# Seven products for eight in the last feed-forward layer of a fused float32 kernel

## The reference, cut to what matters

```python
h2 = rmsnorm_2(x, norm2_g[l])
g = jnp.einsum('bsd,df->bsf', h2, w_gate[l])
u = jnp.einsum('bsd,df->bsf', h2, w_up[l])
x = x + jnp.einsum('bsf,fd->bsd', jax.nn.silu(g) * u, w_down[l])
return rmsnorm_2(x, normf_g)
```

## Time and profile before

| | |
|---|---|
| median of 3 runs | 1824.84 us (1824.78 to 1824.85) |
| span of the profiled execution | 1822.8 us |
| TensorE busy | 1810.1 us, 99% of the span |
| VectorE, ScalarE, GpSimd busy | 938.6, 727.8, 272.3 us |
| the layer's first matmul starts, its last one ends | about 1451.3 and 1811.3 us |

### The profile page before, as it was taken

How to read it: one execution, slowest core, us unless ns; L and a number is a source line. 1 busy time by engine, 2 the same in 40 slices (tenths; PEclk the granted TensorE clock), 3 DMA queues, 4 the chain that set the end, 5 groups by cost and what they waited for, 6 DMA issues and landing times.

```text
span 1822.8 us, 21331 instructions
## 1 busy us (share of the span) xinstructions
PE 1810.1 (99%) x8733; PEld 1472.7 (81%) x8733; DVE 938.6 (51%) x1429; ACT 727.8 (40%) x1155; POOL 272.3 (15%) x241
## 2 busy tenths in 40 slices
...
GB/s 243 67 88 66 70 95 114 93 93 94 91 95 96 118 128 108 82 47 93 93 95 113 93 93 95 91 110 99 70 103 59 70 109 100 93 92 93 102 89 64
DMA packets 32337, 173.41 MB, mean 95 GB/s; under 512 B 4064, under 2 KB 6240, under 8 KB 14320
## 3 DMA queue, kind: packets, MB, share of 16 engines
...
...
## 4 chain that ended last, share of the span: by engine, by line
PE 96%; ACT 1%; DVE 1%; DMA 0%; POOL 0%; issue 0%; SPq 0%; ACTq 0%; DVEq 0%; POOLq 0%
PE ps L995 54%; PE ps L1299 20%; PE ps L929 7%; PE ps L1014 5%; PE ps L1141 2%; PE ps L1186 2%; PE ps L1166 2%; PE ps L1034 1%; PE ps L1225 1%; PE ps L1206 1%; DMA raw<-in_wall 0%; ACT PC L1543 0%; DVE WL L1806 0%; ACT WH L1375 0%; POOL sq L2326 0%
## 5 line engine op out<-in xcount | busy, mean ns | idle before, releaser
L995 PE MATMUL ps<-hH,WH 128*128 128x512 f32 x1456 | 570.9, 392 | 0.1
L1806 DVE TENSOR_TENSOR WL<-raw,WH 128x1024 fp32r<-128x1024 f32 (+2 forms) x308 | 377.3, 1264 | 368.1 <-ACT WH L1375 367.9
L995 PE MATMUL ps<-hH,WL 128*128 128x512 f32 x1456 | 566.7, 389 | 0.0
L995 PE MATMUL ps<-hL,WH 128*128 128x512 f32 x1456 | 566.7, 389 | 0.0
L1375 ACT ACTIVATE WH<-raw 128x1024 fp32r<-128x1024 f32 (+2 forms) x308 | 301.4, 1026 | 311.8 <-PE ps L1299 228.6
L995 PEld LDWEIGHTS ps<-hH,WH 128*128 128x128 f32 x1456 | 273.3, 188 | 65.3 <-issue 7.3
L995 PEld LDWEIGHTS ps<-hH,WL 128*128 128x128 f32 x1456 | 273.3, 188 | 57.0
L995 PEld LDWEIGHTS ps<-hL,WH 128*128 128x128 f32 x1456 | 273.3, 188 | 56.9 <-issue 1.0
L1299 PE MATMUL ps<-fL,WH 128*128 128x512 f32 x531 | 205.9, 388 | 0.0
L1299 PE MATMUL ps<-fH,WL 128*128 128x512 f32 x531 | 205.9, 388 | 0.0
L1299 PE MATMUL ps<-fH,WH 128*128 128x512 f32 x531 | 205.9, 388 | 0.0
...
## 6 DMA issues: line engine op xcount, KB each, us to landing
raw<-in_wall SPq DMA_DIRECT2D x140, 1024.0 KB, 4.6
...
```

The costliest lines, as they stand in the source:

```text
L995: mm = e.matmul(ps[b][:, 0:N], ww[:, k, c:c + 128], x[:, k, 0:N], start=(k == 0 and i == 0), stop=(k == 7 and i == 2))
L1806: e.tensor_tensor(WL[n % NCV][:, c], raw[n % NRAW][:, c], WH[n % NCV][:, c].bitcast(F32), ALU.subtract).then_inc(*mark("wl", n, x))
```

## The change

The last layer's gate and up are made as one 2x2 block product. A round s (of 11) takes 256 columns of gate and 256 of up. The blocks are: k tiles even or odd (4 each), gate or up columns, and tokens 0 to 255 or 256 to 511. The seven products (numbered 1 to 7) use the weight blocks as loaded (1, 2, 4) or sums of them (5, 6, 3, 7), made by VectorE (`wsum`) before the split, and blocks or differences of blocks of the moving side, made once per pair of k tiles in `res_norm`. Each product is 4 x 2 x 3 = 24 matmuls of 256 columns. Products 1, 6, 7, 4 add up in one PSUM bank, 5 and 3 in another, 2 in a third; ScalarE copies the partial sums out (`wcopy`) before the next product is added on top, and the next product waits for that copy. VectorE joins the copies to gate (`wc12`, `wc11`) and up (`wz1`, `wz0`).

Weights are split in chunks of 128x1024, with four places for WH/WL chunks; a chunk is converted when the chunk four before it has been used. A third raw buffer serves the layer. The down product is no longer in two halves: its parts (groups of 2, 4, 4, 4, 4 k tiles, each added to X on its own, `wx`) run between the products, and the last 4 k tiles run as the tail, `res_ffn` as before.

The plan and the order of steps (indentation of the diff is shortened here):

```diff
+WINO = (2,)
+NSU = 11
+CHUNK = 1024
+W_SLOTS = 2 * NCV
+TAIL = ((0, (0,)), (1, (1,)), (2, (2, 3)))
...
+def down_pieces(s):
+  if s == 0:
+    return []
+  if s < 3:
+    return [(0, s - 1)]
+  return [((s - 1) // 2, 2 * ((s - 1) % 2) + x) for x in (0, 1)]
...
+def wino_sequence():
+  out = []
+  for s in range(NSU):
+    q = lambda n, p0=0, p1=4, s=s: ("q", s, n, p0, p1)
+    d = [("d",) + x for x in down_pieces(s)]
+    if s == 0:
+      out += [q(1, 0, 3), q(5, 0, 3), q(2, 0, 3), q(1, 3), q(5, 3), q(2, 3), q(6), q(3), q(7),
+          ("q", 1, 1, 0, 4), q(4)]
+    elif s < 3:
+      out += ([] if s == 1 else [q(1)]) + [q(5), q(6), q(3), q(7), q(2)] + d + [q(4)]
+    else:
+      out += [q(1), q(5), q(6), q(3), d[0], q(7), q(2), d[1], q(4)]
+  return out
...
+units = [ROLE[i, "U1", s], ROLE[i, "U2", s]]
+at = block_of(q)
+if at:
+  c["unit"], c["at"] = ROLE[i, at[0], s], at[1] * CHUNK
+else:
+  c["sum"] = {5: ((units[0], CHUNK), (units[1], 0)), 6: ((i, "q", s, 5), (units[0], 0)),
+        3: ((i, "q", s, 6), (units[1], CHUNK)), 7: ((units[0], 0), (units[0], CHUNK))}[q]
+  c["place"] = {5: 0, 6: 1, 3: 0, 7: 1}[q]
+c["from"] = units[0] if q == 1 else units[1]
...
 def conv_ahead(end):
-  while now["conv"] < min(end, len(UNITS)) and (now["conv"] < NCV or now["conv"] - NCV in done):
-    for x in (0, 1):
-      put("conv", now["conv"], x)
+  while now["conv"] < len(ITEMS):
+    item = ITEMS[now["conv"]]
+    kind, n = item
+    first = n if kind == "unit" else CHUNKS[n]["from"]
+    if first >= end or any((b if b[0] == "chunk" else b[1]) not in done for b in W_BEFORE[item]):
+      return
+    if kind == "unit":
+      for x in (0, 1):
+        put("conv", n, x)
+    else:
+      for c in range(now["summed"], min(n + 2, len(CHUNKS))):
+        if CHUNKS[c]["i"] == CHUNKS[n]["i"]:
+          if CHUNKS[c]["sum"]:
+            put("wsum", c)
+          now["summed"] = c + 1
+      put("cconv", n)
     now["conv"] += 1
...
+def ffn_wino(i, end):
+  late = []
+  def used(key):
+    done.add(("chunk", CHUNK_AT[key]))
+  for at, x in enumerate(SEQUENCE):
+    conv_ahead(len(UNITS))
+    if x[0] == "d":
+      _, g, c = x
+      put("wd", i, g, c)
+      while late:
+        put(*late.pop(0))
+      used((i, "d", g, c))
+      put("wx", i, g, c)
+      continue
+    _, s, q, p0, p1 = x
+    put("wp", i, s, q, p0, p1)
+    while late:
+      put(*late.pop(0))
+    if at == 2:
+      put("rstd_rows", FFN_NORMS[i], 61 if i == 2 else 60)
+    if p1 < 4:
+      continue
+    used((i, "q", s, q))
+    if q in (1, 5, 6, 7):
+      put("wcopy", i, s, q)
+    elif q == 3:
+      put("wc12", i, s)
+    elif q == 2:
+      put("wc11", i, s)
+    if q == (3 if s == 0 else 2):
+      put("wgate", i, s)
+    if q == 4:
+      put("wz1", i, s)
+      late.append(("wz0", i, s))
+  while late:
+    put(*late.pop(0))
+  hread = ("wq", i, NSU - 1, 4)
+  if i == 2:
+    put("sqrt_table")
+  for mg in (0, 1):
+    n = ROLE[i, "T", mg]
+    now["unit"] = n + 1
+    conv_ahead(n + 2)
+    for gi, ks in TAIL:
+      for mi in range(4):
+        put("wtail", i, mg, gi, mi, n, ks)
+        if gi == 2:
+          put("res_ffn", i, 1, 4 * mg + mi, hread)
+    done.add(n)
...
-rstd("n2", 61)
+if 2 not in WINO:
+  rstd("n2", 61)
```

Places, and which moving block a product takes:

```diff
+FH = place("FH", [128, 8, 512], F32R, offset=wino)
+FL = place("FL", [128, 8, 512], F32R, offset=wino + 16384)
+raw.append(place("raw2", [128, SLOT], offset=wino + 32768))
+Wsum = [place(f"Wsum{x}", [128, CHUNK], offset=wino + 40960 + 4096 * x) for x in (0, 1)]
+held_q1, held_q5, held_v, held_w = (place(f"held{x}", [128, 2, 256], offset=wino + 49152 + 2048 * x)
+                  for x in range(4))
+TH = place("TH", [128, 4, 3, 256], F32R, offset=wino + 57344)
+TL = place("TL", [128, 4, 3, 256], F32R, offset=wino + 57344 + 12288)
+gs = place("gs", [128, 2, 512], offset=wino + 81920)
+yz = place("yz", [128, 2, 512], offset=wino + 86016)
+Tf = place("Tf", [128, 8, 256], offset=wino + 81920)
+DH = place("DH", [128, 4, 4, 256], F32R, offset=hH_at)
+DL = place("DL", [128, 4, 4, 256], F32R, offset=hL_at)
...
+def moving(q, p):
+  x = {1: 0, 2: 1, 3: 2, 4: 3, 5: 4, 6: 5, 7: 6}[q]
+  if x < 3:
+    return TH[:, p, x, :], TL[:, p, x, :]
+  return DH[:, p, x - 3, :], DL[:, p, x - 3, :]
```

TensorE:

```diff
+elif what == "wp":
+  i, st, pn, p0, p1 = a
+  c = CHUNK_AT[i, "q", st, pn]
+  kind = {1: "wA", 6: "wA", 7: "wA", 4: "wA", 5: "wD", 3: "wD", 2: "wB"}[pn]
+  opens = pn in (1, 5, 2)
+  if opens and p0 == 0:
+    b, before = bank((kind, i, st), {"wA": ("wg", "z", 0), "wD": ("wg", "c12"), "wB": ("wg", "c11")}[kind] + (i, st),
+            hold=kind == "wA")
+    if before:
+      w.wait_ge(*at(*before))
+  b = BANK[kind, i, st]
+  if not opens:
+    w.wait_ge(*at("wcopy", i, st, {6: 1, 7: 6, 4: 7, 3: 5}[pn]))
+  w.wait_ge(*at("wl", "c", c))
+  W = [x.rearrange("p (k c) -> p k c", k=4) for x in chunk_slot(c)]
+  for p in range(p0, p1):
+    w.wait_ge(*at("wg", "t", "L", i, p, int(pn > 3)))
+    H, L = moving(pn, p)
+    for u in (0, 1):
+      for n, (ww, x) in enumerate(((W[0], H), (W[0], L), (W[1], H))):
+        mm = e.matmul(ps[b][:, 256 * u:256 * u + 256], ww[:, p, 128 * u:128 * u + 128], x,
+               start=(opens and p == 0 and u == 0 and n == 0),
+               stop=(p == 3 and u == 1 and n == 2), skip_group_check=True)
+  if p1 == 4:
+    mm.then_inc(*mark("wq", i, st, pn))
+    FREED["chunk", c] = ("wq", i, st, pn)
+  if pn == 4:
+    turns.append(b)
...
+for mi, m in enumerate(part_tiles(g, part)):
+  b, before = bank(("wd", i, g, m), ("wg", "x", i, g, m))
+  if before:
+    w.wait_ge(*at(*before))
+  for kx in range(nk):
+    f = k0 + kx
+    w.wait_ge(*at("wpool", "L", i, f // 2))
+    for n, (ww, x) in enumerate(((W[0], FH), (W[0], FL), (W[1], FH))):
+      mm = e.matmul(ps[b][:, :], ww[:, kx, mi * 128:mi * 128 + 128], x[:, f % 8, :],
+             start=(kx == 0 and n == 0), stop=(kx == nk - 1 and n == 2))
+  mm.then_inc(*mark("wq", "d", i, g, m))
+  FREED["chunk", c] = ("wq", "d", i, g, m)
```

ScalarE (`cconv`, `wcopy`, the silu of `wgate`, the copy of `wz0`, `res_norm`):

```diff
+elif what == "cconv":
+  c = a[0]
+  if CHUNKS[c]["sum"]:
+    w.wait_ge(*at("wg", "sum", c))
+  else:
+    w.wait_ge(*loaded(CHUNKS[c]["unit"]))
+  for b in W_BEFORE["chunk", c]:
+    w.wait_ge(*at(*FREED[b]))
+  e.activation(chunk_slot(c)[0], chunk_src(c), ACT.Copy).then_inc(*mark("wh", "c", c))
+elif what == "wcopy":
+  i, st, pn = a
+  dst = {1: held_q1, 5: held_q5, 6: held_v, 7: held_w}[pn]
+  w.wait_ge(*at("wq", i, st, pn))
+  if st:
+    w.wait_ge(*at(*{1: ("wg", "c11"), 5: ("wg", "z", "c22"), 6: ("wg", "c12"), 7: ("wg", "z", 1)}[pn], i, st - 1))
+  e.activation(dst[:, :, :], by_tile(BANK["wD" if pn == 5 else "wA", i, st]), ACT.Copy).then_inc(
+    *mark("wcopy", i, st, pn))
+elif what == "wgate":
+  i, st = a
+  if st:
+    w.wait_ge(*at("wpool", "L", i, st - 1))
+  w.wait_ge(*at("wg", "r", i, st))
...
+e.activation(yz[:, :, :], gs[:, :, :], ACT.Silu).then_inc(*mark("wsilu", i, st))
...
+w.wait_ge(*at("wg", "z", 1, i, st))
+w.wait_ge(*at("wg", "z", 0, i, st))
+if st >= 4:
+  w.wait_ge(*at("wq", "d", i, group_of(st - 4), 7))
+f = 2 * st % 8
+e.activation(FH[:, f:f + 2, :], yz[:, :, :], ACT.Copy).then_inc(*mark("wsilu", "H", i, st))
...
+if st in WINO_OF:
+  i, p = WINO_OF[st], m // 2
+  src = X[:, m, :].rearrange("p (h t) -> p h t", h=2)
+  if p:
+    w.wait_ge(*at("wg", "t", "L", i, p - 1, 1))
+  e.activation(Tf[:, 1:3, :] if m % 2 else Tf[:, 0:8:7, :], src, ACT.Copy,
+        scale=col(st, m)).then_inc(*mark("wcopy", "t", "g", i, m))
+  if m % 2:
+    w.wait_ge(*at("wcopy", "t", "g", i, m))
+    e.activation(TH[:, p, :, :], Tf[:, 0:3, :], ACT.Copy).then_inc(*mark("wcopy", "t", "H", i, p, 0))
+    w.wait_ge(*at("wg", "t", "d", i, p, 4))
+    e.activation(DH[:, p, :, :], Tf[:, 3:7, :], ACT.Copy).then_inc(*mark("wcopy", "t", "H", i, p, 1))
+else:
+  e.activation(hH[:, m, :], X[:, m, :], ACT.Copy, scale=col(st, m)).then_inc(
+    *mark("hH", st, m))
```

VectorE (`res_norm` last):

```diff
+elif what == "wsum":
+  c = CHUNKS[a[0]]
+  src = []
+  for y in c["sum"]:
+    if len(y) == 2:
+      w.wait_ge(*loaded(y[0]))
+      src.append(raw[RAW_AT[y[0]]][:, y[1]:y[1] + CHUNK])
+    else:
+      w.wait_ge(*at("wg", "sum", CHUNK_AT[y]))
+      src.append(Wsum[CHUNKS[CHUNK_AT[y]]["place"]][:, :])
...
+  e.tensor_tensor(Wsum[c["place"]][:, :], src[0], src[1], ALU.add).then_inc(*mark("wg", "sum", a[0]))
+elif what == "cconv":
+  c = a[0]
+  H, L = chunk_slot(c)
+  w.wait_ge(*at("wh", "c", c))
+  e.tensor_tensor(L, chunk_src(c), H.bitcast(F32), ALU.subtract).then_inc(*mark("wl", "c", c))
...
+elif what == "wc11":
+  i, st = a
+  w.wait_ge(*at("wq", i, st, 2))
+  w.wait_ge(*at("wcopy", i, st, 1))
+  if st:
+    w.wait_ge(*at("wsilu", i, st - 1))
+  e.tensor_tensor(gs[:, :, 0:256], by_tile(BANK["wB", i, st]), held_q1[:, :, :], ALU.add).then_inc(
+    *mark("wg", "c11", i, st))
+elif what == "wgate":
+  i, st = a
+  w.wait_ge(*at("rrow", FFN_NORM[i]))
+  w.wait_ge(*at("wg", "c11", i, st))
+  w.wait_ge(*at("wg", "c12", i, st))
+  R = Rsb[:, :].rearrange("p (o t) -> p o t", o=1).broadcast_to([128, 2, 512])
```

(61 more changed lines are left out.)

284 lines of the change are left out of this document (249 added, 35 removed).

## The result

The change makes the kernel slower: 1856.0 us median of 4 runs (1853.9 to 1856.2) beside 1824.8 (1824.6 to 1824.9) in the same session, ratio 1.0169, 95% interval [1.0154, 1.0183]. The forecast had the sign, but 1835 for the size; 1856 is 8 us outside the range.

The account below looks back on a forecast made before the run. TensorE, busy 1810.1 of 1822.8 us, was taken as the bound. A 17.7 us saving against losses at the start, in the rounds, by clock and at the end summed to +10.4: span 1833.2, time 1835 us; 80% range 1824 to 1848.

Parts of the forecast that it names:

- Pace: TensorE in gate and up: 1848 matmuls of 256 columns at 0.120 us replace 1056 of 512, saving 17.7 us.
- rival E: Products' matmuls follow at half the 512-column pace, 0.1134 us, weight loads hiding better: 12.2 us less, 1823; chance 0.03.
- The start: From the attention's output tiles through product 4 of round 0: TensorE waits for VectorE's late list, +14.1 us (9 to 18).
- Round 2: VectorE's string from product 2 to the next product 1's copy takes 17.9 us for 14.08: +3.8 (0 to 5).
- Round 3: The wait before product 6 there, from a VectorE string of 15.9 us for 14.08: +1.8 (0 to 5).
- Steady: Later rounds: string from product 2 to the next product 1's copy barely fits; 0.3 us lost in each of 7, +2.1.
- Clock: TensorE at half rate for one block of 18 matmuls after the start's second long wait: +1.9 us (0 to 3.8).
- Last FL: Last round's end: GpSimd's FL is done at 9.2 us where TensorE wants it at 8.3: +0.9 (0 to 2).
- Tail acc: After the last large matmul: VectorE's per-tile string falls behind, acc of tile 6 ends later, +1.9 us (1 to 2.2).
- B: Rival: steady string does not fit, through 2x256 copies or GpSimd's share; 1.4 us more in 7 rounds, 1845; chance 0.28.
- D: Rival: no change within 0.2%; waits echoing into rounds 1 to 3 don't come and the clock holds, 1826; chance 0.11.
- C: Rival: VectorE's list keeps up at the start, so the 10.3 us of waits there go: 1820.8, faster; chance 0.08.

## Why the prediction was right and wrong

- **Pace, -17.7:** right. 24 matmuls of a product take 2.88 us, 0.120 each; rival E is out.
- **The start, +14.1:** 15.9 (0.9 before tile 6, 5.9, 5.4, 1.6, 2.0). Each wait is where it was forecast, ended by what the walk named (before product 3 of round 0 the prediction's list of signs says a copy; it is chunk 3, as in its walk). The walk left out GpSimd's adds of squares; with these gone product 5 starts at the forecast 1464.
- **Round 1, +1.6:** 1.4. **Round 2, +3.8:** 5.8. **Round 3, +1.8:** 3.4. **Steady, +2.1:** 6.9. Here is the step that failed, in the prediction's words: "GpSimd's 2.55 us (Y) beside it adds up to 0.5". It adds 1.4: 13.6 becomes 15.0 for 14.08 us of room, 0.9 a round. Without Y round 2's wait falls from 5.8 to 4.5 and round 3's from 3.4 to 2.3; what is left over the forecast in these two (0.7 and 0.5) is not traced. The rows in hand were a mean (1302 ns) and a pair of 2.66, read as an instruction a little slower beside GpSimd, where it was one that met GpSimd's last 0.4 us (it began at 1447.21, GpSimd's add of 1446.31 ran 1.34). Leaving Y out and moving it to VectorE both show it.
- **Clock, +1.9:** 11.6 with the end's. The fall was foreseen, its spread not: I charged 18 matmuls after one wait, at 0.107 us each, and it is 17 to 25 after each of five, at 0.093. By size this is the larger miss, 9.7 of the 21 us, but it follows from the waits: the one of round 3, which the term above lengthened, brings no half clock without Y. By itself, with extra matmuls in the waits, 6.4 came back.
- **Last FL, +0.9:** 1.1. **Tail acc, +1.9:** 1.9.
- **Rivals.** B has the steady string too long, as it was (1.0 us lost a round, where the forecast had 0.3 and B 1.4 more), but its first reason is wrong: the copies with 2x256 patterns take 0.58 us as plain ones; its second, GpSimd's share, is the true one; the time lies above its range too. D falls: the echoes came, larger than charged, and the clock did not hold. C falls: it needed the start's waits away, and even the reordered start keeps some. The slack of 0 to 0.5 us fits the runs without Y, and so small that one standstill overran it.

The forecast would have been 1835 + 4.8 (steady) + 3.6 (rounds 2, 3) + 1.8 (start) + 9.7 (clock) = 1854.9 with the measured terms, 1.1 under the 1856.0.
